# Two-block layer on one core: turns among products, rotary tables made once, loads reordered

## The reference

```python
# first block
h = rmsnorm(x, norm1_g);  p = h @ w_in                     # 1024 -> 2560
u, dq, dk, dv, sq, sk, sv = split(p)                       # 256, 3 x 512, 3 x 256
mix = concat(pool_mixer(u), diff_attention(dq, dk, dv),    # 4 causal heads, two softmaxes each
             stick_breaking_attention(sq, sk, sv))         # 4 causal heads
x = x + mix @ w_out
h2 = rmsnorm(x, norm2_g)
x = rmsnorm(x + (silu(h2 @ w_gate) * (h2 @ w_up)) @ w_down, final_norm_g)   # 1024 -> 2816 -> 1024
# second block
shift, scale, gate = split(silu(c) @ w_ada + b_ada)        # one row each
h = rmsnorm_2(x, g_pre) * (1 + scale) + shift
gu, gv, gg, rq, rk, rv, rg = split(h @ w_in_2)             # 7 x 512
y = concat(gmlp_branch(gu, gv, gg), retention_branch(rotary(rq, positions), rotary(rk, positions), rv, rg))
out = x + gate * rmsnorm_2(y @ w_out_2, g_post)

def rotary(x, positions):                                  # per token and frequency
    ang = positions * 10000 ** (-i / 64)                   # i = 0..63
    return concat(x1 * cos(ang) - x2 * sin(ang), x2 * cos(ang) + x1 * sin(ang))
```

## Time and profile before

| | |
|---|---|
| median of 3 runs | 4122.55 us (4120.18 to 4125.41) |
| the profiled execution's own time, its span | 4125.86 us, 4123.6 us |
| mean granted PE clock | 0.964 |
| busy: PE, PEld, DVE, ACT, POOL | 3780.3 us (92%), 3379.4 (82%), 2012.1 (49%), 1709.7 (41%), 801.5 (19%) |
| chain that ended last | PE 48%, DVE 10%, ACT 4%, DMA 2%, issue 2%, SPq 1% |
| mean traffic | 187 GB/s |

### The profile page before, as it was taken

How to read it: one execution, slowest core, us unless ns; L and a number is a source line. 1 busy time by engine, 2 the same in 40 slices (tenths; PEclk the granted TensorE clock), 3 DMA queues, 4 the chain that set the end, 5 groups by cost and what they waited for, 6 DMA issues and landing times.

```text
span 4123.6 us, 59429 instructions
## 1 busy us (share of the span) xinstructions
PE 3780.3 (92%) x23304; PEld 3379.4 (82%) x23304; DVE 2012.1 (49%) x4385; ACT 1709.7 (41%) x3467; POOL 801.5 (19%) x704
## 2 busy tenths in 40 slices
PE   8989898999998889999998989999998989999898
PEld 7778788777777788888888988788878889888797
DVE  3446564556655555556545545444566543111433
ACT  3334454546644444455544333434554433111322
POOL 3433333444443331100011000110000000000100
PEclk9989999999999999999999999999999999999999
DMA  6785566676664557545453455454453345555443
GB/s 188 249 264 178 179 209 218 245 250 227 240 237 166 189 186 271 186 167 172 150 184 127 171 184 197 152 188 176 143 185 112 113 169 204 184 184 204 153 161 137
DMA packets 330855, 772.97 MB, mean 187 GB/s; under 512 B 36561, under 2 KB 219857, under 8 KB 274258
## 3 DMA queue, kind: packets, MB, share of 16 engines
q1 hardware_dynamic: 269522, 729.31, 50.9%
q10 hardware_dynamic: 61056, 39.86, 3.4%
HBM read 590.54 MB, written 178.54 MB: 187 GB/s over the span
## 4 chain that ended last, share of the span: by engine, by line
PE 48%; DVE 10%; ACT 4%; DMA 2%; issue 2%; SPq 1%; POOL 0%; DVEq 0%; ACTq 0%
PE PS L1243 13%; PE PS L1245 13%; PE PS L1244 13%; PE PS L1348 2%; PE PS L1334 2%; DMA GROW<-in_gmlp_ln_g 2%; PE PS L1326 1%; PE PS L1325 1%; PE PS L1350 1%; DVE PT L1868 1%; DVE PP L1899 1%; DVE SM L1836 1%; DVE GB L1755 0%; ACT PT L1563 0%; SPq L2350 0%
## 5 line engine op out<-in xcount | busy, mean ns | idle before, releaser
L1243 PE MATMUL PS<-WF,BIG 128*128 128x256 f32 x2768 | 810.0, 293 | 34.4 <-ACT XS L1626 9.1
L1244 PE MATMUL PS<-WF,BIG 128*128 128x256 f32 x2768 | 795.9, 288 | 0.0
L1245 PE MATMUL PS<-WF,BIG 128*128 128x256 f32 x2768 | 795.1, 287 | 0.0
L1243 PE MATMUL PS<-BIG,WF 128*128 128x512 f32 (+1 forms) x1792 | 693.0, 387 | 27.7 <-ACT BIG L1505 11.8
L1245 PE MATMUL PS<-BIG,WF 128*128 128x512 f32 (+1 forms) x1792 | 679.5, 379 | 0.0
L1244 PE MATMUL PS<-BIG,WF 128*128 128x512 f32 (+1 forms) x1792 | 678.7, 379 | 0.0
L2136 POOL TENSOR_TENSOR WF<-RAW,WF 128x512 fp32r<-128x512 f32 x380 | 508.2, 1360 | 828.6 <-ACT WF L1448 828.4
L1243 PEld LDWEIGHTS PS<-WF,BIG 128*128 128x128 f32 x2768 | 542.7, 196 | 49.0 <-ACT XS L1626 9.5
L1244 PEld LDWEIGHTS PS<-WF,BIG 128*128 128x128 f32 x2768 | 543.5, 196 | 7.7 <-issue 2.3
L1245 PEld LDWEIGHTS PS<-WF,BIG 128*128 128x128 f32 x2768 | 542.8, 196 | 0.0
L1868 DVE TENSOR_TENSOR PT<-PS,PT 128x512 fp32r<-128x512 f32 (+3 forms) x320 | 195.1, 610 | 589.2 <-ACT PT L1563 588.5
(11 more groups left out here) (222 smaller groups left out, 6869.4 us busy)
## 6 DMA issues: line engine op xcount, KB each, us to landing
WF<-scratch_WS SPq DMA_DIRECT2D x264, 1024.0 KB, 5.0
scratch_WS<-WF SPq DMA_DIRECT2D x110, 1024.0 KB, 6.5
W<-scratch_WS SPq DMA_DIRECT2D x66, 1024.0 KB, 5.0
RAW<-in_w_in SPq DMA_DIRECT2D x84, 512.0 KB, 4.3
KV<-scratch_KS SPq DMA_DIRECT2D x60, 512.0 KB, 5.7
KV<-scratch_VS SPq DMA_DIRECT2D x60, 512.0 KB, 5.0
QQ<-scratch_QS SPq DMA_DIRECT2D x192, 128.0 KB, 5.0
XH<-in_x SPq DMA_DIRECT2D x32, 512.0 KB, 6.0
```

The source lines that it names most:

```text
L1243: pe.matmul(o, Ah, Bh, start=first, stop=False)
L1244: pe.matmul(o, Ah, Bl, start=False, stop=False)
L1245: return pe.matmul(o, Al, Bh, start=False, stop=last)
```

## The change

1. **Next stage's first turns.** Chunk c+1's first-pair turns (for the last chunk, those of w_out's input) are issued inside the last v unit of chunk c's projection (`turn_next`), rounds 0 to 2 after its first tile v and round 3 after its second.
2. **Second pair's turns among products.** From chunk 1 on, the projection's first `f_block` runs rounds 0 and 1 after the first unit's part 0, and rounds 2 and 3 after the second's. In w_out's first `t_block`, rounds 0 to 2 come after the last first-pair unit's tile 0 and round 3 after its tile 1. The feed-forward's turns and those of kind "pre" stay where they were.
3. **Start.** The first two tiles of x and two half blocks of weights are loaded before the second two tiles; squares and norm of the second pair come behind the first pair's turns.
4. **Rotary tables.** Angles, sines and cosines of all 16 tiles are made once, in the first chunk's projection (after blocks 1 to 4), in the attention's buffer PP, and stored to scratch memory TB; `load_tables` loads 128x256 of each per chunk. The attention's first use of PP waits for the store.
5. **Loads.** b_ada's and g_post's rows are loaded early into ROW and OB. The loads of w_out's first input come after block 8 of the last chunk's projection instead of behind it.

```diff
-        def flush(held=0):
-            while late:
-                late.pop(0)(held)
+        def flush(held=0, kps=range(4)):
+            for turn in late:
+                turn(held, kps)
+            if kps[-1] == 3:
+                del late[:]
...
+            if first:
...
+                for f, (u, b, before) in enumerate(banks):
+                    do(("gemm_f", u, w, f, 0, range(8), b, before, rd))
+                    yield 2.9
+                    if ready and not f:
+                        flush(0, (0, 1))
+                flush(2, (2, 3) if ready else range(4))
...
+                        second = ready and not g and w == ws[-1]
+                        if second and not v:
+                            flush(0, range(3))
+                        elif second:
+                            bank.skip(1)
+                            flush(0, (3,))
...
         def ada_steps():
+            do(("load_ada_rows",))
...
+        def turn_next(c):
+            rd, made = (("n1", c + 1), scaled("n1", c + 1, 0)) if c < NC - 1 else (("y", 0), (("y", 0, 0),))
+            return lambda kps: turn_round(rd, 0, made, rd[0], (("mm", mm["n"] - 2),), kps=kps)
+        first_norm(0)
+        turn_round(("n1", 0), 0, scaled("n1", 0, 0), "n1", ())
         for c in range(NC):
             rd = ("n1", c)
-            turn_round(rd, 0, scaled("n1", c, 0), "n1", big_free[0])
...
+                if (c, nblk) == (0, 0):
+                    first_norm(1)
+                    split_half()
...
-                    for cost in t_block([w], rd, [done]):
+                    for cost in t_block([w], rd, [done], turn_next(c) if nblk == 9 else None):
...
-                    for cost in f_block(w, rd, nblk == 0, done):
+                    for cost in f_block(w, rd, nblk == 0, done, False, c > 0):
...
+                if c == 0 and nblk in (1, 2, 3, 4):
+                    do((("load_positions", "angles", "rotary_tables", "store_tables")[nblk - 1],))
+                if (c, nblk) == (NC - 1, 8):
+                    yield "att", 0
+                    for g in range(2):
+                        load_y(0, g)
...
-                        if not nun and count == 8:
-                            do(("angles", c, at_last))
-                        if not nun and count == total:
-                            do(("rotary_tables", c))
...
-        pch = Ring(10)
+        pch = Ring(10, [(("tables",),)] * 10)
...
+            def load_ada_rows():
+                sp.dma_start(ROW[:, :], I["b_ada_2"][0:1, 2048:3072].broadcast_to([128, 1024])).then_inc(*landed("s_rbl", ("rbl",)))
+                sp.dma_start(OB[:, :], I["g_post_2"][0:1, :].broadcast_to([128, 1024])).then_inc(*landed("s_rgl", ("rgl",)))
...
+            def load_positions():
+                sp.dma_start(invf, const[:, C_INVF:C_INVF + 64]).then_inc(*landed("s_pos", ("pos",)))
+                sp.dma_start(posi, I["positions_2"][0, :].rearrange("(t p) -> p t", p=128),
+                             allow_slow_non_contiguous=True).then_inc(*landed("s_pos", ("pos",)))
```

More of the change, by code:

```diff
@@ L302, in released, with f_block @@
             fetch_halves()
-        def f_block(w, rd, first, done, joint=False):
+        def f_block(w, rd, first, done, joint=False, ready=False):
             banks = []
+            if first:
+                for f in range(2):
+                    u = unit()
+                    banks.append((u,) + bank.take(done("frees", f, u, None)))
+                for f, (u, b, before) in enumerate(banks):
[5 more added lines that the diff above has]
+                split_half()
+                for f, (u, b, _) in enumerate(banks):
+                    do(("gemm_f", u, w, f, 1, range(8), b, (), rd))
+                    done("do", f, u, b)
+                    yield 2.9
+                released(w, 0, ("mm", u))
+                released(w, 1, ("mm", u))
+                return
             for f in range(2):
@@ L309, in f_block, with t_block @@
                 b, before = bank.take(done("frees", f, u, None))
-                banks.append((u, b))
-                if first:
-                    do(("gemm_f", u, w, f, 0, range(8), b, before, rd))
-                    yield 2.9
-                else:
-                    do(("gemm_f", u, w, f, None, range(4), b, before, rd))
-                    if f:
-                        released(w, 0, ("half", u))
-                    yield 2.8
-                    do(("gemm_f", u, w, f, None, range(4, 8), b, (), rd))
-                    done("do", f, u, b)
-                    if f == 0 or joint:
-                        split_half(joint)
-                    yield 2.8
-            if first:
-                flush(2)
-                split_half()
-                for f, (u, b) in enumerate(banks):
-                    do(("gemm_f", u, w, f, 1, range(8), b, (), rd))
-                    done("do", f, u, b)
-                    yield 2.9
-                released(w, 0, ("mm", banks[1][0]))
-            released(w, 1, ("mm", banks[1][0]))
-        def t_block(ws, rd, dones, ahead=None, parts=(range(8),)):
+                do(("gemm_f", u, w, f, None, range(4), b, before, rd))
+                if f:
+                    released(w, 0, ("half", u))
+                yield 2.8
+                do(("gemm_f", u, w, f, None, range(4, 8), b, (), rd))
+                done("do", f, u, b)
+                if f == 0 or joint:
+                    split_half(joint)
+                yield 2.8
+            released(w, 1, ("mm", u))
+        def t_block(ws, rd, dones, ahead=None, parts=(range(8),), ready=False):
             for g in range(2):
-                if g:
+                if g and late:
                     flush()
@@ L392, in projections @@
         do(("start",))
-        for t in range(4):
+        for t in range(2):
             do(("load_x", "n1", 0, t, ()))
-            if t < 2:
-                do(("constants_first", t))
-        for _ in range(3):
+            do(("constants_first", t))
+        for _ in range(2):
             load_half()
+        for t in (2, 3):
+            do(("load_x", "n1", 0, t, ()))
+        load_half()
         do(("load_constants",))
@@ L402, in projections, with load_y, first_norm @@
         us_all = (("zero", 1),)
-        for g in range(2):
+        y_free = {0: (("xp", ("n1", 3), 1, 7),), 1: (("xp", ("n1", 3), 1, 7),)}
+        def load_y(c, g):
+            do(("load_y", c, g, pool_stored[c] + tuple(att_stored[c]) + y_free[g]))
+        def first_norm(g):
             for t in (2 * g, 2 * g + 1):
@@ L1103, in build @@
         RSTD = smc(112, 16)
-        POSF, ONE = smc(192, 4), smc(200, 1)
+        ONE = smc(200, 1)
         BN, MV = smc(208, 24), smc(256, 8)
@@ L1613, in ada, with rotary_tables @@
                     act.preload_act_table_set(EXP_LN)
[L1615 to L1619 removed]
+            def rotary_tables():
+                on.wait_ge("ang")
+                act.activation(sin_all, cos_all, ACT.Sin).then_inc(*inc("sines", ("sn", 0)))
+                on.wait_ge("sn", 0)
+                act.activation(cos_all, cos_all, ACT.Sin, scale=0.5).then_inc(*inc("sines", ("sn", 1)))
                 act.preload_act_table_set(EXP_LN)
```

101 lines of the change are left out of this document (43 added, 58 removed).

## The result

| | before | changed |
|---|---|---|
| median, us | 4122.64 (4120.18 to 4125.41), 4 runs | 4091.48 (4087.98 to 4094.75), 3 runs |
| ratio of changed to before, 95% interval | | 0.9924 (0.9905 to 0.9944) |
| the profiled execution's own time, its span | 4125.86, 4123.6 | 4091.48, 4089.7 |
| mean granted PE clock | 0.964 | 0.964 |

A fourth run of the changed kernel took 6062.62 us at a mean clock of 0.555 and is in neither the median nor the ratio; with it the median would be 4093.11. The kernel became faster by 31.2 us where 59 were forecast.

A forecast was written before the change was run, and what follows sets the result against it. PE, busy 3780.3 of 4123.6 us, was taken to wait on other engines' queues. The terms summed to −59.0, from 4125.86 to 4066.9; with the median 3.3 lower, the forecast was 4063.6, range 4045 to 4092.

The forecast's parts named there:

- The start: First product: the first two weight roundings go ahead of the second pair's steps and begin about 3 us earlier; −3.
- Tables in the first chunk: First chunk's projection: angles on DVE and sines on ACT delay weights and so PE; +9, bounds 0 and +16.
- rival 4: First chunk: DVE stands at the cast until the positions' load lands, holding up PE; slower, 4132 just past that point; chance 0.03.
- Starts of the chunks: Projection starts of second to fourth chunk: idle time and low clock shrink; −5.5, −6 and −3.
- rival 2: Projection's new places gain nothing, ACT's stores and weights still precede the second pair's evictions; 4078; chance 0.14 with another rival.
- Rows of ada: Product at 275.12: the wait of 6.43 for late rows and the low clock behind it mostly go; −8.
- w_out's first input: Start of w_out: the earlier load ends the 11.83 wait, transposes and products run at better clock; −14.4.
- w_out's second-pair turns: Turns among w_out's first products in four chunks: −7.4 together, less allowance for new waits, −4.6 (+3 to −9).
- the bank that is skipped: In w_out: with DVE's additions of x, it can make the new places wait 0.7 each.
- Angles and sines: "Pre" turns lose waits behind angle instructions, −20 (−14 to −23); retention loses waits behind sines, −3.5 (0 to −8).
- Rival 1: Gains turn into other waits, PE reaching attention whose DVE chain is late; half comes back, 4093; chance 0.2.

The follow-up runs named there:

- e4: Changed kernel with the angles cut into eight steps over the first chunk's blocks, sines and table store moved to the second chunk's projection: 4077.22 us, ratio 0.9886 to before.
- e9: The changed kernel itself, unaltered, measured again: 4101.06 us, ratio 0.9935 to the kernel before.
- e8: Changed kernel with the second pair's turns of the projection's first block (chunks 2 to 4) together again behind both first parts: 4094.84 us, ratio 0.9926 to before.
- e6: Kernel before, with only the row loads of b_ada and g_post moved early: 4123.45 us, ratio 0.9998 to before.
- e11: Changed kernel without any moved turns (next stage's first, projection's, w_out's); tables, early loads and start order stay: 4103.39 us, ratio 0.9950 to before.
- e7: Changed kernel without the first pair's turns in the projection's last unit, w_out's early input load kept: 4113.80 us, ratio 0.9970 to before.
- e10: Changed kernel without the turns among w_out's first products, and without the single bank skip that goes with them: 4089.87 us, ratio 0.9910 to before.
- e12: As e5, but in place of its bank skips the turns among w_out's products are taken out: 4072.97 us, ratio 0.9865 to before.
- e2: Kernel before, with one single bank skip per chunk's feed-forward, moving the ring as the change does: 4131.46 us, ratio 1.0015 to before.
- e1: Changed kernel with three single bank skips added per chunk's feed-forward, putting the ring back where it was: 4075.86 us, ratio 0.9882 to before.
- e5: Changed kernel with bank skips restoring the ring, attention's first loads two weight loads sooner and angles in eight steps: 4061.32 us, ratio 0.9849 to before.
- e3: Changed kernel with attention's first four loads (keys, values, queries) issued two weight loads sooner: 4083.42 us, ratio 0.9894 to before.

## Why the prediction was half right

The direction was right and the size half: −59.0 forecast, −34.4 in the profiled execution, −31.2 in the medians. The time is inside the range by 0.5 us only, at its end. By the prediction's own steps, in the profiled execution:

- **The start**, −3: measured −3.6, and −4.8 by product 73. Right.
- **Tables in the first chunk**, +9 (0 to +16): +12.5 by product 625, by the chain that was described (9.1 of it by product 553), and up to 15.5 in other executions. The term was too small. The chain's own pieces were near (DVE held for 13.4 instead of 11.6); what was counted at 0 without a reason is the traffic of the store and the row loads, in a stretch whose DMA engines were at a share of 0.93, and weight loads did land 2.5 to 4.8 us later there. How much of the loss is theirs is open (e4, e9). The positions (rival 4) were in time.
- **Starts of the chunks**, −5.5, −6, −3: −6.2, −5.5 and −2.2, 13.9 of 14.5. Right in size. The explanation, that ACT's stores stand ahead of the second pair's evictions and limit the gain, goes with what happened only in part: the second pair's new places added nothing (e8), so rival 2's mechanism was there, without its price, since the first pair's new place is enough.
- **Rows of ada**, −8: −10.4 between products 745 and 1249, the remaining wait 1.41 as forecast, and +8.1 right behind it. This step failed. The prediction said what stays (a chain of 1.5 us) and not what PE reaches next: attention's first queries, whose load SP can issue only behind a weight load. e6 measured the whole at 0 (−5 to +3).
- **w_out's first input**, −14.4: −12.9 between products 2641 and 2689, the wait being 0.48. Right in size; but by e11 and e7 the early load alone gives 4.4 to 5.4 of it and the turns the rest.
- **w_out's second-pair turns**, −4.6: the turns themselves gave more, 8 to 9 over the four chunks (e10, e12), the forecast's −7.4 before its allowance for new waits. But "the bank that is skipped" was priced at a local wait of 0.7, and it moved the ring of banks for the rest of the stage: 15.8 at the four "pre" places, 9.0 (e2) to 13.4 (e1) when what comes back behind them is counted, 6 (2 to 10) by e2's ratio. This is the largest miss. The order of instructions alone did not show it, for no row moves; the bank's number does.
- **Angles and sines**, −20 and −3.5: with the ring where it was, the four stretches gain 23.1 to 26.0 (e1, e5, e10, e11, e12). Right, and confirmed without a moved turn (25.5 in e11). In the changed kernel the same stretches show −12.6, because the ring's price lies in them.
- **Rival 1**, the gains turned into other waits, gave 4093, and 4091.5 is the time measured; but that is luck, for its mechanism, attention waiting for DVE, fell: that wait shrank from 44.5 to 39.5. The waits that came are one load, one ring and late weights, and each could be taken away (e3, e1, e4). (Its "30 of the 59 us" won at a load, late rows or vanished steps is not what the terms give: 14.4, 8, 20 and 3.5 are 45.9.)

So the forecast failed in two terms that looked only at the place of the edit, the skipped bank and the rows of ada, and was too low in a third, the tables. What remains open: the changed kernel's two medians differ by 10 us, and in its profile 4.3 us between products 2089 and 2641 and 5.1 between product 16033 and the end were lost with no edit near.

## What to carry to other kernels

A skip in a ring of buffers is not local: it changes who waits for whom in every later unit that takes from the ring or assumes where it stands, so look up the buffer numbers at the next places with hard-wired ones, or skip on to the full circle where buffers are long free. When a wait is removed, ask what the engine reaches next and when that was issued; here 8 of 8 us came back 8 us later from a load queued behind another load that waited. One-time work was cheap in pieces of 0.7 to 3.6 us (under 2 us lost in e4, e5 and e12) and dear in one piece of 13 (12 to 15 lost) on an engine that feeds another one in order. Two moves that mend the same wait do not add up: here either kind of turn at the chunk starts was worth 7 us or more alone, and the second nothing beside the first.

## What the runs showed of the hardware

The 16 products of 64 columns by a column of scalars took 4.90 us in one piece, though by the same form's busy time, 3.0 us for 16, they were put at 3.0. Fourteen of them take 0.25 us each and start 0.16 apart, as before the change; the last two take 1.37 and 1.33. Cut in two (e5; e4 is the same to 0.01), the first eight took 1.40 us and the second eight 3.56, and again it is the last two of the sixteen, 1.35 and 1.31, though they run 11 us later. So it goes with these two tiles or their scalars rather than with what runs beside. The cast of 16 columns took 1.26 us, that of 4 columns 0.16:

```profile
63.45 1.26 DVE L2011 CAST PP<-PP 128x16 f32<-128x16 int32 x1
64.74 1.40 DVE L2014 TENSOR_SCALAR PP<-PP 128x64 f32<-128x64 f32 x8
76.77 3.56 DVE L2014 TENSOR_SCALAR PP<-PP 128x64 f32<-128x64 f32 x8
```

The fused step of 1024 columns, which I took at 1.54, took 1.25 here (5.00 for four). The cause of the two slow products and of the slow cast was not tried.
